# Differential attention: VectorE copies the turned probabilities out of PSUM, GpSimd forms the difference for the first 128 queries

## The chip, the cores and the metric

The kernel runs on one core of a Trainium2 chip. The metric is the device time of one execution in microseconds (us); the figure given is the median of three runs. The engines are named as the profile names them: TensorE (PE, with PEld for its weight loads), VectorE (DVE), ScalarE (ACT), GpSimd (POOL) and SyncE (SP). Each engine works through its own instructions in the order in which they are written, and semaphores hold one engine back for another.

## The reference, cut to what matters

The model is four transformer layers of width 1024 over 256 tokens, with an attention of one of three kinds between two feed-forward parts, and two more layers of another kind behind them. The change touches the two layers (the first and the fourth) that use differential attention: 8 heads, each with two sets of scores, whose softmaxes are subtracted before they meet the values.

```python
def diff_attention(h, w_in, w_out, lam, subln_g, lambda_init, pos):
    q, k, v = jnp.split(h @ w_in, 3, axis=-1)
    ...
    lam_full = jnp.exp(jnp.sum(lam[0] * lam[1])) - jnp.exp(jnp.sum(lam[2] * lam[3])) + lambda_init
    ...
        sc = jnp.einsum('bqhcd,bkhcd->bhcqk', qc, k, preferred_element_type=jnp.float32) * scale
        p = masked_probs(sc, pos[None, :] <= qpos[:, None])
        a = p[:, :, 0] - lam_full * p[:, :, 1]
        return jnp.einsum('bhqk,bkhe->bqhe', a.astype(v.dtype), v)

    o = chunked(chunk, S // Q_BLOCK)
    o = rms_norm(o, subln_g, DIFF_SUBLN_EPS) * (1.0 - lambda_init)
    return o.reshape(B, S, H * DIFF_V_DIM) @ w_out
```

## The kernel before, in words

Every engine's program is written by hand, and the order of the calls is the order of its instructions. Most of the time goes into large matrix products: the weights stream in by DMA, ScalarE and VectorE split each weight into a high and a low part (tiles HI and LO), and TensorE multiplies both. Between the input product of an attention and its output product (function `rows_of_outputs`, whose matmuls are at L826) lies the core of the attention, a pipeline over the 8 heads; the change lies there, in both differential layers.

In that core, for head i, TensorE computes two score matrices (`pair_scores`, L892, and the mask added at L900), into PSUM, of 384 columns each: columns 0 to 127 hold queries 0 to 127 against keys 0 to 127, columns 128 to 383 hold queries 128 to 255 against all 256 keys. VectorE finds the negated row maxima (`maxima`, tile NM, L2141 and L2142). ScalarE takes the exponentials into SBUF (`exps`, tile SB, L1614) with their row sums. VectorE inverts the sums (`reciprocals`, tile RC, L2146), makes one factor for each query (tile CF, L2192), and forms first set plus factor times second set in place, in two instructions (L2197): one over the 128 columns of the first group of queries, one over the other 256. TensorE turns the 128 by 128 blocks of the result (`probs_turned`, L706) into PSUM bank 4. ScalarE copies the turned blocks into SBUF (`probs`, tile PT, L1622). TensorE multiplies them with the values (`outputs`, L923; `mixed` in the program). ScalarE sums the squares of the output (`sums`, L1450), GpSimd makes the inverse root from them (`outputs_roots`, L2611 and L2613), and VectorE scales the output into its place (`in_place`, L2205 and L2208).

The heads overlap. TensorE's order in round i is: scores of head i+2, turn of head i, output of head i-1. VectorE's is: difference of head i, `in_place` of head i-3, maxima of head i+2. ScalarE's is: copy of head i, exponentials of head i+2, squares of head i-1. In round 7 TensorE also turns the finished first half of the output (`outputs_flipped`), which ScalarE and VectorE split into a high and a low part (`outputs_high`, `outputs_low`, tiles XH and XL). The output product at L826 begins when head 5 is in its place and this first half is split. GpSimd has done its part in moving queries and keys (`exchange`) long before; in the core it makes only the inverse roots.

Of the kernel before, what the change touches and what calls it, by code (L numbers as in the profile page):

```python
# [122 lines left out]
def build(nc, a, out, mods, turned, turned_qk):  # L123
    ctx = ExitStack()
    with ctx:
# [20 lines left out]
        def sem(name):  # L146
            return ctx.enter_context(nc.semaphore(name))
# [205 lines left out]
        s_cf = sem("s_cf")  # L353
        s_df = sem("s_df")
        s_d0 = sem("s_d0")
        s_p1 = sem("s_p1")
# [138 lines left out]
        for st in steps:  # L495
# [89 lines left out]
            "sc": pair, "ma": {"mix2": 4}, "nm": soft, "ex": soft, "rc": soft,  # L585
            "cf": {"diff": 8}, "df": {"diff": 8, "nsa": 16}, "p1": {"nsa": 16}, "d0": {"nsa": 16}, "pf": soft, "pt": soft, "mix": pair,
            "eq": {"diff": 16, "mix2": 16}, "ev": {"diff": 8, "mix2": 4}, "er": {"diff": 8, "mix2": 4},
# [10 lines left out]
        def bank_of(i):  # L598

            return (6, 4)[i] if i < 2 else 2 * ((i + 1) % 2)  # L600
# [96 lines left out]
        def _(e):  # L697
# [264 lines left out]
            def softmax_attention(st):  # L962
# [19 lines left out]
                for i in range(8):  # L982
                    if i + 2 < 8:

                        e.wait_ge(*((s_cp, c["cp"] + 5 + i) if i < 2 else (s_ex, c["ex"] + i + 1)))
                        if i == 2:
                            e.wait_ge(s_qt, c["qa"] + 4)
                        pair_scores(st, i + 2)
                    if i == 0:

                        e.wait_ge(s_ex, c["ex"] + 2)
                    if i == 7:

                        e.wait_ge(s_ex, c["ex"] + 8)
                        outputs_flipped(st, 0, 8 if diff else 4)
                    e.wait_ge(s_df if diff else s_ex, c["df" if diff else "ex"] + i + 1)
                    probs_turned(st, i, nj)
                    if i >= 1:
                        mixed(i - 1)
# [413 lines left out]
        def _(e):  # L1413
# [203 lines left out]

            def probs(st, i, nj):
                e.wait_ge(s_pf, st.c["pf"] + i + 1)
                if i >= 2:  # L1620
                    e.wait_ge(s_mix, st.c["mix"] + i - 1)
                e.activation(st.t["PT"][:, i % 2, 0:nj, :], ps[:, 4:4 + nj, 0:384], ACT.Copy).then_inc(s_pt, 1)  # L1622

# [9 lines left out]
            def diff_or_moba(st):  # L1633
# [29 lines left out]
                for i in range(8):  # L1663
                    if i == 7:
                        outputs_high(st, 0)
                    probs(st, i, 1 if diff else 2)
                    if i + 2 < 8:
                        exps(st, i + 2, bank_of(i + 2))
                    if diff and i >= 1:
                        sums(i - 1)  # L1670
# [196 lines left out]
        def _(e):  # L1867
# [297 lines left out]
            def diff(st):  # L2165
# [20 lines left out]
                def difference(i):  # L2186

                    reciprocals(st, i)
                    if i == 0:
                        e.wait_ge(s_lam, c["lam"] + 4)  # L2190
                    e.wait_ge(s_rc, c["rc"] + i + 1)
                    e.scalar_tensor_tensor(out=CF[:, i], in0=SM[:, i, :, 0], scalar=LS[:, 5:6], in1=RC[:, i, :, 1],  # L2192
                                           op0=ALU.mult, op1=ALU.mult).then_inc(s_cf, 1)
                    e.wait_ge(s_cf, c["cf"] + i + 1)
                    X = SB[:, i % 3]
                    for t, (c0, c1) in enumerate(((0, 128), (128, 384))):
                        o = e.scalar_tensor_tensor(out=X[:, 0, c0:c1], in0=X[:, 1, c0:c1], scalar=CF[:, i, t:t + 1],  # L2197
                                                   in1=X[:, 0, c0:c1], op0=ALU.mult, op1=ALU.add)
                    o.then_inc(s_df, 1)

# [13 lines left out]
                projected(st, 5, TM, 0, 0)  # L2214
                maxima(st, 2, bank_of(2))
                maxima(st, 3, bank_of(3))
                for i in range(2, 8):
                    difference(i)
                    if i >= 3:
                        in_place(i - 3)  # L2220
                    if i == 7:
                        outputs_low(st, 0)
                    if i + 2 < 8:
                        maxima(st, i + 2, bank_of(i + 2))
                for i in range(5, 8):
# [274 lines left out]
        def _(e):  # L2500
# [104 lines left out]

            def outputs_roots(st, width, eps, at, pairs):

                for i in range(pairs):
                    ss, v, r = (ST[:, at + 3 * width * i + j * width:at + 3 * width * i + (j + 1) * width] for j in range(3))
                    e.wait_ge(s_eq, st.c["eq"] + width * (i + 1))  # L2610
                    e.tensor_scalar(v, ss, 1.0 / P, eps, ALU.mult, ALU.add).then_inc(s_ev, 1)  # L2611
                    e.wait_ge(s_ev, st.c["ev"] + i + 1)
                    e.tensor_tensor(r, v, NH[:, 0:width], ALU.pow).then_inc(s_er, 1)  # L2613

            def diff(st):
# [5 lines left out]
                exchange(st, 4)  # L2621
                outputs_roots(st, 2, 1e-5, 32, 8)

# [25 lines left out]
            def mix2(st):  # L2649
# [8 lines left out]
                exchange(st, 2)  # L2658
                outputs_roots(st, 4, 1e-6, 32, 4)
                load_for(bounds[st.k + 1])  # L2660
# [50 lines left out]
```

## Time and profile before

| what | value |
| --- | --- |
| device time, median of 3 runs (lowest to highest) | 2737.24 us (2736.77 to 2737.26) |
| the profiled execution: span from first to last instruction | 2735.8 us |
| TensorE busy in it | 2707.6 us, 99% of the span |
| VectorE, ScalarE, GpSimd busy | 1939.9, 1541.6, 533.0 us |
| first differential layer's core, by the output product's start | up to 286.49 us |
| second differential layer's core, by the output product's start | up to 1761.85 us |

The span is the profiled execution's own time; the median of the runs lies 1.4 us above it, for what lies around the instructions. A busy share of 99% for TensorE is an average over the whole program: in the cores of the attentions it is lower, and what happens there is read from those stretches alone. Every time in the text below that has no other unit is in microseconds from the start of the span, or a duration in microseconds.

### The profile page before, as it was taken

How to read it: one execution, taken by the hardware profiler on the slowest of the kernel's cores; microseconds unless marked ns; L12 is line 12 of the kernel's file. 1: busy time of each engine (PE TensorE's matmuls, PEld its weight loads, DVE VectorE, ACT ScalarE, POOL GpSimd, SP SyncE). 2: the span in 40 equal slices, each digit the busy share in tenths (PEclk: the TensorE clock that was granted, in tenths of full speed). 3: DMA queues.
4: the chain of work that ended last, by engine and by line, in shares of the span. 5: the costliest groups of instructions: out<-in, count | busy, mean ns of one | idle time of the engine just before them, and what ended most of it. 6: DMA issues, size and time to landing. Idle time of an engine off the chain costs nothing.

```text
span 2735.8 us, 34478 instructions
## 1 busy us (share of the span) xinstructions
PE 2707.6 (99%) x12754; PEld 2216.3 (81%) x12754; DVE 1939.9 (71%) x2831; ACT 1541.6 (56%) x2646; POOL 533.0 (19%) x930
## 2 busy tenths in 40 slices
PE   9999999999999999999999999999999999999998
PEld 7887788888888888876888888788788788788787
DVE  6877777787667778767786787778764765745764
ACT  6547764654766465456654656765445444444543
POOL 3211221221112122115221211122110021110120
PEclk9999999999999999999999999999999999999999
DMA  9867488786748868661796886478675686764773
GB/s 293 288 229 256 155 273 281 223 280 234 254 144 275 288 215 281 242 211 50 226 292 226 272 305 226 155 250 292 238 238 186 202 264 219 247 196 166 235 244 114
DMA packets 386919, 633.87 MB, mean 232 GB/s; under 512 B 25760, under 2 KB 255136, under 8 KB 386496
## 3 DMA queue, kind: packets, MB, share of 16 engines
q1 hardware_dynamic: 350752, 535.02, 58.9%
q0 software_dynamic: 35856, 96.30, 11.0%
q8 instruction: 101, 1.65, 0.2%
q14 instruction: 66, 0.54, 0.1%
q10 hardware_dynamic: 144, 0.36, 0.0%
HBM read 593.26 MB, written 38.32 MB: 231 GB/s over the span
## 4 chain that ended last, share of the span: by engine, by line
PE 95%; DVE 3%; ACT 1%; issue 1%; POOL 0%; DMA 0%; DVEq 0%; ACTq 0%
PE ps L736 41%; PE ps L826 28%; PE ps L742 20%; PE ps L706 2%; PE ps L892 1%; PE ps L923 1%; PE ps L795 1%; ACT SB L1614 1%; PE ps L933 0%; DVE M L2026 0%; PE ps L900 0%; ACT JUNK L1450 0%; PE ps L1065 0%; DVE H L1972 0%; DVE M L1969 0%
## 5 line engine op out<-in xcount | busy, mean ns | idle before, releaser
L736 PE MATMUL ps<-HI,XH 128*128 128x512 f32 x2480 | 973.2, 392 | 1.7 <-DVE LO L1886 0.8
L736 PE MATMUL ps<-LO,XH 128*128 128x512 f32 x2480 | 966.5, 390 | 0.0
L1881 DVE TENSOR_TENSOR LO<-RAW,HI 128x1024 fp32r<-128x1024 f32 x468 | 564.6, 1218 | 328.9 <-ACT HI L1430 326.6
L742 PE MATMUL ps<-HI,XL 128*128 128x512 f32 x2480 | 767.5, 391 | 0.4
L1430 ACT ACTIVATE HI<-RAW 128x1024 fp32r<-128x1024 f32 x468 | 492.7, 1060 | 483.2 <-PE ps L826 279.5
L1886 DVE SCALAR_TENSOR_TENSOR LO<-RAW,GC,HI 128x512 fp32r<-128x512 f32 (+1 forms) x896 | 617.0, 742 | 142.2 <-ACT HI L1437 141.0
L1437 ACT ACTIVATE HI<-RAW,GC 128x512 fp32r<-128x512 f32 (+1 forms) x896 | 586.3, 713 | 206.5 <-PE ps L742 177.6
L736 PEld LDWEIGHTS ps<-HI,XH 128*128 128x128 f32 x2480 | 466.1, 188 | 103.4 <-DVE LO L1886 3.1
L742 PEld LDWEIGHTS ps<-HI,XL 128*128 128x128 f32 x2480 | 464.1, 188 | 105.2 <-DVE XL L1922 9.7
L736 PEld LDWEIGHTS ps<-LO,XH 128*128 128x128 f32 x2480 | 466.5, 188 | 94.5
L2583 POOL DMA_DIRECT2D AX<-turned x440 | 240.0, 552 | 351.3 <-DMA turned<-AT 302.9
L826 PE MATMUL ps<-HI,AH 128*128 128x512 f32 x856 | 265.2, 391 | 0.0
L826 PE MATMUL ps<-LO,AH 128*128 128x512 f32 x856 | 263.8, 389 | 0.0
L826 PE MATMUL ps<-HI,AL 128*128 128x512 f32 x856 | 263.8, 389 | 0.0
L826 PEld LDWEIGHTS ps<-HI,AL 128*128 128x128 f32 x856 | 160.7, 188 | 33.5
L826 PEld LDWEIGHTS ps<-LO,AH 128*128 128x128 f32 x856 | 160.7, 188 | 33.4
L826 PEld LDWEIGHTS ps<-HI,AH 128*128 128x128 f32 x856 | 159.6, 188 | 32.5
L2578 POOL DMA_DIRECT2D turned<-AT x110 | 61.9, 563 | 532.4 <-DVE AT L2087 532.4
L1566 ACT ACTIVATE SG<-ps,ST 128x256 f32<-128x256 f32 x176 | 73.7, 471 | 129.6 <-PE ps L742 129.6
L2529 POOL TENSOR_TENSOR ST<-ST,NH 128x1 f32<-128x1 f32 x56 | 34.5, 617 | 518.9 <-DVE ST L2005 263.5
L2078 DVE SCALAR_TENSOR_TENSOR AF<-ps,ST,SG 128x256 f32<-128x256 f32 x176 | 77.0, 480 | 80.2 <-ACT SG L1566 80.2
L1916 DVE SCALAR_TENSOR_TENSOR ACC<-RAW,CS,ACC 128x512 f32<-128x512 f32 x168 | 126.1, 751 | 5.1
(229 smaller groups left out, 2210.4 us busy)
## 6 DMA issues: line engine op xcount, KB each, us to landing
RAW<-in_ffn_w_in SPq DMA_DIRECT2D x350, 512.0 KB, 5.1
RAW<-in_ffn_w_out SPq DMA_DIRECT2D x88, 1024.0 KB, 6.2
RAW<-in_w_ada SPq DMA_DIRECT2D x48, 1024.0 KB, 6.6
RAW<-in_w_in SPq DMA_DIRECT2D x44, 1024.0 KB, 5.2
RAW<-in_w_ffn_in SPq DMA_DIRECT2D x88, 512.0 KB, 4.9
turned<-AT POOLq DMA_DIRECT2D x110, 256.0 KB, 2.6
AX<-turned POOLq DMA_DIRECT2D x440, 64.0 KB, 3.6
RAW<-in_diff_w_in SPq DMA_DIRECT2D x24, 1024.0 KB, 5.4
```

Source lines behind the costliest of these rows:

```text
L736: e.matmul(ps[:, b + t, 0:nw], XH[:, k, t * P:(t + 1) * P], q[s][:, c * nw:(c + 1) * nw], start=(k == 0 and q is HI), stop=False)
L742: i = e.matmul(ps[:, b + t, 0:nw], XL[:, k, t * P:(t + 1) * P], HI[s][:, c * nw:(c + 1) * nw], start=False, stop=(k == 7))
L826: i = e.matmul(ps[:, 4 + 2 * t + nh, :], x(k, t), q[s][:, nh * 512:nh * 512 + 512], start=(k == 0 and q is HI and x is th), stop=(k == chu ...
L1430: e.activation(HI[n % NSPLIT][:, 0:t.width], RAW[t.buf][:, h * t.width:(h + 1) * t.width], ACT.Copy).then_inc(s_hi, 1)
L1437: i = e.activation(HI[n % NSPLIT][:, c * w:(c + 1) * w], RAW[t.buf][:, h * t.width + c * w:h * t.width + (c + 1) * w], ACT.Copy, scale=g[c])
L1566: o = e.activation(SG[:, i, t], ps[:, b + t, 0:S], ACT.Silu, scale=r)
L1881: e.tensor_tensor(LO[n % NSPLIT][:, 0:w], RAW[t.buf][:, at[1] * w:(at[1] + 1) * w], HI[n % NSPLIT][:, 0:w].bitcast(F32), ALU.subtract).the ...
L1886: i = e.scalar_tensor_tensor(out=LO[n % NSPLIT][:, c * w2:(c + 1) * w2], in0=RAW[t.buf][:, at[1] * w + c * w2:at[1] * w + (c + 1) * w2], s ...
L1916: e.scalar_tensor_tensor(out=A, in0=src, scalar=CS[:, kc:kc + 1], in1=A, op0=ALU.mult, op1=ALU.add).then_inc(s_ada, 1)
L2078: o = e.scalar_tensor_tensor(out=AF[:, i, t], in0=ps[:, b + t, S:2 * S], scalar=root_of(st, t)[0], in1=SG[:, i, t], op0=ALU.mult, op1=ALU. ...
L2578: e.dma_start(rows, AT[:, g % 2, :]).then_inc(s_bw[g % 2], 16)
L2583: e.dma_start(AX[32 * c:32 * c + 32, g % 3, :].rearrange("p (q n) -> p q n", q=4), rows[:, c * P:(c + 1) * P].rearrange("(q j) n -> j q n" ...
```

## The change

Three pieces of work change hands in the two differential layers. The copy of the turned probabilities out of PSUM goes from ScalarE to VectorE (`turned_copied`), behind the maxima of head i+2. The difference of the first 128 queries goes from VectorE to GpSimd, where it takes two instructions with a wait between them: a scaling in place of the second set's 128 columns, then an addition. TensorE's turn of a head now waits for both engines. In VectorE's order the maxima of head i+2 come before `in_place` of head i-3, where they came behind it. GpSimd makes the roots of head i-2 behind the difference of head i. Nothing else moves; the result is the same sum.

```diff
@@ TensorE, softmax_attention
                     e.wait_ge(s_df if diff else s_ex, c["df" if diff else "ex"] + i + 1)
+                    if diff:
+                        e.wait_ge(s_d0, c["d0"] + i + 1)
                     probs_turned(st, i, nj)
@@ ScalarE, diff_or_moba
                 for i in range(8):
                     if i == 7:
                         outputs_high(st, 0)
-                    probs(st, i, 1 if diff else 2)
+                    if not diff:
+                        probs(st, i)
@@ VectorE, diff
                     X = SB[:, i % 3]
-                    for t, (c0, c1) in enumerate(((0, 128), (128, 384))):
-                        o = e.scalar_tensor_tensor(out=X[:, 0, c0:c1], in0=X[:, 1, c0:c1], scalar=CF[:, i, t:t + 1],
-                                                   in1=X[:, 0, c0:c1], op0=ALU.mult, op1=ALU.add)
-                    o.then_inc(s_df, 1)
+                    e.scalar_tensor_tensor(out=X[:, 0, 128:384], in0=X[:, 1, 128:384], scalar=CF[:, i, 1:2],
+                                           in1=X[:, 0, 128:384], op0=ALU.mult, op1=ALU.add).then_inc(s_df, 1)
+
+                def turned_copied(i):
+
+                    e.wait_ge(s_pf, c["pf"] + i + 1)
+                    if i >= 2:
+                        e.wait_ge(s_mix, c["mix"] + i - 1)
+                    e.tensor_copy(x["PT"][:, i % 2, 0, :], ps[:, 4, 0:384]).then_inc(s_pt, 1)
...
                 maxima(st, 2, bank_of(2))
+                turned_copied(0)
                 maxima(st, 3, bank_of(3))
+                turned_copied(1)
                 for i in range(2, 8):
                     difference(i)
+                    if i + 2 < 8:
+                        maxima(st, i + 2, bank_of(i + 2))
+                    turned_copied(i)
                     if i >= 3:
                         in_place(i - 3)
                     if i == 7:
                         outputs_low(st, 0)
-                    if i + 2 < 8:
-                        maxima(st, i + 2, bank_of(i + 2))
@@ GpSimd, diff
-                outputs_roots(st, 2, 1e-5, 32, 8)
+                SB, CF = st.t["SB"], st.t["CF"]
+                for i in range(10):
+                    if i < 8:
+
+                        e.wait_ge(s_cf, st.c["cf"] + i + 1)
+                        X = SB[:, i % 3]
+                        e.tensor_scalar(X[:, 1, 0:P], X[:, 1, 0:P], CF[:, i, 0:1], None, ALU.mult).then_inc(s_dm, 1)
+                        e.wait_ge(s_dm, st.c["cf"] + i + 1)
+                        e.tensor_tensor(X[:, 0, 0:P], X[:, 0, 0:P], X[:, 1, 0:P], ALU.add).then_inc(s_d0, 1)
+                    if i >= 2:
+                        output_roots(st, 2, 1e-5, 32, i - 2)
```

VectorE's instructions for head 5 in the first differential layer stood as follows before the change. RC, SM and CF are reciprocals, row sums and factors, SB the exponentials, M the output.

```order
L2146 RECIPROCAL RC_99<-SM_98 128x4 [waits s_ex]
L2192 SCALAR_TENSOR_TENSOR CF_104<-SM_98,LS_106,RC_99 128x2 [waits s_rc]
L2197 SCALAR_TENSOR_TENSOR SB_95<-SB_95,CF_104 128x128 [waits s_cf]
L2197 SCALAR_TENSOR_TENSOR SB_95<-SB_95,CF_104 128x256
L2205 TENSOR_TENSOR ST<-ST,RC_99 128x2 [waits s_er]
L2208 SCALAR_TENSOR_TENSOR M<-ps,ST,SGN_107 128x128 [waits s_ef]
L2208 SCALAR_TENSOR_TENSOR M<-ps,ST,SGN_107 128x128
L2141 TENSOR_REDUCE NM_97<-ps 128x2 [waits s_sc]
L2142 TENSOR_REDUCE NM_97<-ps 128x2
```

The same round of the changed kernel on VectorE (its own line numbers):

```order
L2150 RECIPROCAL RC_99<-SM_98 128x4 [waits s_ex]
L2196 SCALAR_TENSOR_TENSOR CF_104<-SM_98,LS_106,RC_99 128x2 [waits s_rc]
L2200 SCALAR_TENSOR_TENSOR SB_95<-SB_95,CF_104 128x256 [waits s_cf]
L2145 TENSOR_REDUCE NM_97<-ps 128x2 [waits s_sc]
L2146 TENSOR_REDUCE NM_97<-ps 128x2
L2208 COPY PT_96<-ps 128x384 [waits s_mix,s_pf]
L2214 TENSOR_TENSOR ST<-ST,RC_99 128x2 [waits s_er]
L2217 SCALAR_TENSOR_TENSOR M<-ps,ST,SGN_107 128x128 [waits s_ef]
L2217 SCALAR_TENSOR_TENSOR M<-ps,ST,SGN_107 128x128
```

One of the two instructions on SB is gone, the two maxima have moved ahead, and a copy that waits for TensorE's turn of the same head (s_pf) stands in the middle of the round, with `in_place` and the next head's difference behind it.

On GpSimd, the first differences of a layer now stand directly behind the last DMAs that `exchange` issues, where the first root stood.

```order
L2610 DMA turned_qk<-AT_102 128x1024 [waits s_qa]
L2615 DMA AX_103<-turned_qk 32x4x256 [waits s_qw,s_qt]
L2615 DMA AX_103<-turned_qk 32x4x256 x3
L2639 TENSOR_SCALAR SB_95<-SB_95,CF_104 128x128 [waits s_cf]
L2641 TENSOR_TENSOR SB_95<-SB_95 128x128 [waits s_dm]
```

Eight such pairs of a TENSOR_SCALAR and a TENSOR_TENSOR are new in each of the two layers, and from the third on the two instructions of a root follow each pair.

## Rows read from the trace of the kernel before

**Rows 1.** The page's first line.
```profile
span 2735.8 us, 34478 instructions
```

**Rows 2.** Stretches: length, busy PE, PEld, DVE, ACT, POOL (instructions), clock, DMA share, GB/s.
```profile
274.00:280.00 6.00, 3.94 (x34) 2.96 (x34) 5.75 (x20) 6.00 (x30) 2.27 (x5) 1.00 0.00 0
280.00:284.00 4.00, 3.42 (x17) 3.42 (x18) 3.12 (x12) 3.59 (x16) 1.49 (x5) 0.60 0.00 0
1750.00:1756.00 6.00, 3.95 (x34) 2.96 (x34) 5.75 (x20) 6.00 (x30) 2.27 (x5) 1.00 0.01 1
```

**Rows 3.** Chain that ended last, first layer: start, us, what.
```profile
279.78 0.76 DVE SB L2197 x2
...
280.58 0.76 PE ps L706 x3
```

**Rows 4.** Timeline, second layer, round 5: start, us, instruction, [idle before <-releaser].
```profile
1752.24 0.53 ACT L1622 ACTIVATE PT<-ps 128x384 f32<-128x384 f32 x1
1752.72 0.37 ACT L1614 ACTIVATE SB<-ps,NM 128x128 f32<-128x128 f32 x1
1752.75 0.22 DVE L2192 SCALAR_TENSOR_TENSOR CF<-SM,LS,RC 128x2 f32<-128x2 f32 x1
1753.01 0.75 DVE L2197 SCALAR_TENSOR_TENSOR SB<-SB,CF 128x128 f32<-128x128 f32 x2
1753.27 0.48 DVE L2197 SCALAR_TENSOR_TENSOR SB<-SB,CF 128x256 f32<-128x256 f32 x1
1753.67 0.15 DVE L2205 TENSOR_TENSOR ST<-ST,RC 128x2 f32<-128x2 f32 x1
1753.81 0.55 PE L706 MATMUL ps<-CST,SB 128*128 128x128 f32 x3 [0.35 <-DVE SB L2197]
1754.39 0.41 DVE L2141 TENSOR_REDUCE NM<-ps 128x2 f32<-128x256 f32 x1
1755.31 0.17 DVE L2146 RECIPROCAL RC<-SM 128x4 f32<-128x4 f32 x1
1755.52 0.22 DVE L2192 SCALAR_TENSOR_TENSOR CF<-SM,LS,RC 128x2 f32<-128x2 f32 x1
```

**Rows 5.** Timelines of another attention's core: VectorE's copy, GpSimd's scalings, what overlaps.
```profile
1242.48 0.17 DVE L2276 TENSOR_TENSOR CG<-RC,GS 128x4 f32<-128x4 f32 x1
1242.74 1.02 POOL L2646 TENSOR_SCALAR SB<-SB,CG 128x256 f32<-128x256 f32 x1 [0.87 <-DVE CG L2276]
1243.74 0.60 POOL L2646 TENSOR_SCALAR SB<-SB,CG 128x128 f32<-128x128 f32 x1
...
1245.56 0.55 DVE L2286 COPY PT<-ps 128x384 f32<-128x384 f32 x1
1246.03 0.41 DVE L2141 TENSOR_REDUCE NM<-ps 128x2 f32<-128x256 f32 x1
1247.00 0.92 POOL L2646 TENSOR_SCALAR SB<-SB,CG 128x256 f32<-128x256 f32 x1
1247.38 0.41 DVE L2346 TENSOR_TENSOR PC<-PC,MC 128x240 f32<-128x240 f32 x1
```

**Rows 6.** GpSimd's groups by form: count, busy us, mean ns, idle before.
```profile
L2613 POOL TENSOR_TENSOR ST<-ST,NH 128x2 f32<-128x2 f32 x16 | 11.2, 700 | 1.3
L2611 POOL TENSOR_SCALAR ST<-ST 128x2 f32<-128x2 f32 x16 | 3.1, 193 | 58.8 <-ACT JUNK L1450 58.7
```

**Rows 7.** Timeline: head 2's factor and the output product's start, both layers; XL.
```profile
268.57 0.22 DVE L2192 SCALAR_TENSOR_TENSOR CF<-SM,LS,RC 128x2 f32<-128x2 f32 x1
286.49 0.47 PE L826 MATMUL ps<-HI,XH 128*128 128x512 f32 x1 [0.17 <-issue]
1744.57 0.22 DVE L2192 SCALAR_TENSOR_TENSOR CF<-SM,LS,RC 128x2 f32<-128x2 f32 x1
1759.76 1.28 DVE L1922 TENSOR_TENSOR XL<-ps,XH 128x512 fp32r<-128x512 f32 x2
1761.85 0.47 PE L826 MATMUL ps<-HI,XH 128*128 128x512 f32 x1 [0.53 <-issue]
```

More of the change, by code:

```diff
@@ L354, in build @@
         s_df = sem("s_df")
+        s_dm = sem("s_dm")
         s_d0 = sem("s_d0")
@@ L585, in build @@
             "sc": pair, "ma": {"mix2": 4}, "nm": soft, "ex": soft, "rc": soft,
-            "cf": {"diff": 8}, "df": {"diff": 8, "nsa": 16}, "p1": {"nsa": 16}, "d0": {"nsa": 16}, "pf": soft, "pt": soft, "mix": pair,
+            "cf": {"diff": 8}, "df": {"diff": 8, "nsa": 16}, "p1": {"nsa": 16}, "d0": {"diff": 8, "nsa": 16}, "pf": soft, "pt": soft, "mix": pair,
             "eq": {"diff": 16, "mix2": 16}, "ev": {"diff": 8, "mix2": 4}, "er": {"diff": 8, "mix2": 4},
@@ L1616, in exps, with probs @@
                 o.then_inc(s_ex, 1)
-            def probs(st, i, nj):
+            def probs(st, i):
                 e.wait_ge(s_pf, st.c["pf"] + i + 1)
@@ L1621, in probs @@
                     e.wait_ge(s_mix, st.c["mix"] + i - 1)
-                e.activation(st.t["PT"][:, i % 2, 0:nj, :], ps[:, 4:4 + nj, 0:384], ACT.Copy).then_inc(s_pt, 1)
+                e.activation(st.t["PT"][:, i % 2], ps[:, 4:6, 0:384], ACT.Copy).then_inc(s_pt, 1)
             def outputs_high(st, half):
@@ L2604, in exchange, with output_roots @@
                                     turned_qk[q][:, c * S:(c + 1) * S].rearrange("(q j) n -> j q n", q=4)).then_inc(sem_r, 16)
[L2606 to L2613, printed above, removed]
+            def output_roots(st, width, eps, at, i):
+                ss, v, r = (ST[:, at + 3 * width * i + j * width:at + 3 * width * i + (j + 1) * width] for j in range(3))
+                e.wait_ge(s_eq, st.c["eq"] + width * (i + 1))
+                e.tensor_scalar(v, ss, 1.0 / P, eps, ALU.mult, ALU.add).then_inc(s_ev, 1)
+                e.wait_ge(s_ev, st.c["ev"] + i + 1)
+                e.tensor_tensor(r, v, NH[:, 0:width], ALU.pow).then_inc(s_er, 1)
             def diff(st):
@@ L2658, in mix2 @@
                 exchange(st, 2)
-                outputs_roots(st, 4, 1e-6, 32, 4)
+                for i in range(4):
+                    output_roots(st, 4, 1e-6, 32, i)
                 load_for(bounds[st.k + 1])
```

## The prediction, as it was put on record before the run

> **What bounds the kernel now.** I started from the page: the span is 2735.8 us [rows 1], so one profiled execution lies 1.4 us under the median of 2737.24, and the sum below is made against the span and carried over with those 1.4. TensorE is busy nearly all the time, so a change in an attention's core counts only as far as it lengthens or shortens TensorE's idle time there. Next I asked for busy time by stretch in the cores of the two layers [rows 2]. In the steady part of the first (274 to 280) TensorE works 3.94 of 6.00 us, VectorE 5.75 and ScalarE 6.00; the second layer shows the same three numbers. TensorE is not the bound there; VectorE and ScalarE are both nearly full. The chain that ended last goes in the first layer from VectorE's difference straight to TensorE's turn [rows 3]: the turn waits for VectorE.
>
> Which of the two full engines sets the pace is seen in one round of the timeline [rows 4]. VectorE's starts follow each other without a gap: factor at 1752.75, difference at 1753.01 and 1753.27, in_place at 1753.67, maxima at 1754.39, reciprocal at 1755.31, next factor at 1755.52. The steps are 0.26, 0.26, 0.40, 0.72, 0.92 and 0.21; they add up to the round of 2.77 us. Nothing in that list waits for another engine, while TensorE's turn sat idle 0.35 us for VectorE's difference. ScalarE's copy and what it waits for take 0.48 of its round (1752.24 to 1752.72). So VectorE sets the pace and ScalarE is close behind.
>
> **The change part by part.** ScalarE loses the copy, 0.48 us per head. As ScalarE follows VectorE, this by itself is worth nothing on the path.
>
> VectorE loses the 128-column difference, a step of 0.26 [rows 4], and gains a copy of 128x384 from PSUM. The very same copy stands in another attention's core: it takes 0.55, and the next instruction starts 0.47 after it [rows 5]. So VectorE's own work goes from 2.77 to 2.77 - 0.26 + 0.47 = 2.98 per round, on the engine that sets the pace, before any wait.
>
> The larger part is a new wait. The copy of head i stands in VectorE's queue before in_place and the next head's difference, and it needs TensorE's turn of the same head, which now needs GpSimd too. Let T be the start of the factor CF of head i.
> - The factor is ready at T + 0.22 [rows 4]. GpSimd starts 0.09 after a VectorE result (1242.48 + 0.17 to 1242.74) [rows 5]: T + 0.31.
> - The scaling: GpSimd's TENSOR_SCALAR with a factor per row takes 0.60 over 128 columns when it follows another; over 256 columns 1.02 as the first after a wait against 0.92 otherwise, so 0.10 more for the first [rows 5]. 0.70: T + 1.01. Its own wait costs another hop of 0.09: T + 1.10.
> - The addition of two 128-column tiles stands nowhere in this trace. From below: a TENSOR_SCALAR over 2 columns with constants takes 0.19. From above: it reads as many elements as the 256-column scaling, 1.02 after a wait [rows 5, 6]. In between lies the fixed 0.19 plus 126 columns at the slope of the scalings, (0.92 - 0.60)/128 = 0.0025 us each, which is 0.51; GpSimd's only two-tile operation, a power over 2 columns, takes 0.70 [rows 6], but a power works more per element than an addition. I take 0.55: T + 1.65.
> - TensorE starts 0.05 after what it waits for (1753.01 + 0.75 to 1753.81) and takes 0.55 to turn three blocks [rows 4]: T + 2.25. With the same hop of 0.05 VectorE's copy starts at T + 2.30.
>
> VectorE, for its part, comes to the copy at T + 0.26 + 0.40 + 0.92 = T + 1.58. It stands 0.72 idle. From the copy: 0.47, in_place 0.72, reciprocal 0.21: the next factor starts at T + 3.70. The round grows from 2.77 to 3.70. That the maxima were moved ahead of in_place gives the wait a cover of 0.92; without it the idle time would be 1.64. In rounds 6 and 7 there are no maxima to cover it, and the round does not get shorter by them as it does now. Late next are TensorE's output of the head, which needs the copied tile, and at the end of the core the output product. The roots that now stand behind each pair on GpSimd cost nothing: the pair and a root (0.19 and 0.70 [rows 6]) fill 2.4 of 3.7 us, and in_place uses a root two rounds later. The first two copies stand behind maxima which wait for TensorE's scores anyway, with GpSimd idle; I cost them at nothing, and if that cover were gone they would cost 0.5 each.
>
> The length of a core, from the factor of head 2 to the first matmul of the output product, is now 286.49 - 268.57 = 17.92 in the first layer and 1761.85 - 1744.57 = 17.28 in the second [rows 7]. After the change: round 2 has no in_place, so 3.70 - 0.72 = 2.98; rounds 3 to 6 take 3.70 each, together 17.78 to the factor of head 7. From there: copy done and in_place of head 4 by 3.49, the low halves 1.28 (XL, [rows 7]), in_place of head 5 0.72, and some 0.1 for its end and the hop: 5.6. In all 23.4. That is 5.5 more in the first layer and 6.1 more in the second, 11.6 together.
>
> The granted clock is the last term. In the first layer's core it reads 0.60 on average from 280 to 284, right behind the stretch in which TensorE was busy 3.94 of 6.00 [rows 2]. The two levels are 1.2 and 2.4 GHz, so some 3.2 of these 4 us ran at the lower one. The second layer's stretch with the same activity stayed at 1.00 [rows 2], and its core is 0.64 shorter. After the change TensorE is idle more, in both layers. I take a fall in both, at 1 us each, and take off the 0.64 already paid: 1.4 more. The bounds are nothing (0.64 won back) and 1.6 in each layer, if all of such a fall lay in TensorE's own work.
>
> Sum: 2735.8 + 11.6 + 1.4 = 2748.8 for the span, and with the 1.4 around it 2750 us, slower by 0.5%.
>
> **The rivals.** *The scaling starts later.* VectorE's remaining difference reads two tiles from SBUF and starts 0.05 before GpSimd's scaling. If one shuts the other out of SBUF, the scaling begins only at its end, T + 0.74 instead of T + 0.31; with 0.43 in six places (five rounds and the end) of two layers that is 5.2 more: 2755. Against it: VectorE's operation on two SBUF tiles at 1247.38 takes 0.41 and lies wholly inside a scaling of GpSimd's (1247.00 to 1247.92), which takes 0.92 as the one behind another does [rows 5]. The Trainium skill (SBUF — State Buffer, Who interferes with whom) states that a VectorE instruction with two SBUF inputs and a GpSimd instruction that reads SBUF exclude each other, the one issued first blocking the other. By that rule the result would be this rival's; the pair at 1247.38 does not bear it out.
>
> *No new wait matters.* If the pair were done in 0.62, TensorE's turn would end before VectorE reaches its copy, and only VectorE's own 2.98 would count: rounds of 2.26, three of 2.98 and one of 2.06, together 13.3, and an end of 4.7: 18.0, which is 0.1 and 0.7 more than now. With the clock as it is: 2738. Against it: the scaling alone takes 0.70.
>
> *Faster.* ScalarE also shows 6.00 of 6.00 [rows 2], and if it set the pace, its 0.48 less would shorten the five rounds from 2.77 to 2.29 in each of two layers, 4.8, and its copy of the last head would leave the end, another 0.5 each: 2731.5. It decides from the point where VectorE's round falls below 2.77, so it needs both a pair under 0.62 and a copy step under 0.26, where the rows show 0.70 and 0.47.
>
> *The clock stays low longer*, into the output product: beyond 1.6 a layer, over 2757.
>
> For the addition's own price the Trainium skill has a figure: GPSIMD Engine Reference, Elementwise — side-by-side cycle accounting, gives 4497 ns for such an addition over 2048 columns, which scaled to 128 is an estimate of 0.28 us without a fixed cost. By it the sum would be 0.27 x 12 = 3.2 less, 2747; no row here shows it.
>
> **How the numbers follow.** Forecast 0.74, the scaling shut out 0.14, no wait 0.06, faster 0.03, a longer low clock 0.03. About 0.2%, 5.5 us, is what a measurement of this kernel can tell from no change. The addition between 0.19 and 1.02 moves the sum by -0.36 x 12 = -4.3 and +0.47 x 12 = +5.6; the clock by -2.0 and +1.2. Both ends at once give 2743.7 to 2756.8; I give 2743 to 2757, which holds the shut-out scaling too and leaves out no wait, faster and the long low clock. Slower 0.74 + 0.14 + 0.03 = 0.91; the same 0.06; faster 0.03.
>
> **What would show it.** In the changed profile: VectorE's copy idle about 0.7 us before most heads and 1.6 in rounds 6 and 7, released by TensorE's turn; the turn released by GpSimd's addition, not by VectorE; the pair at 0.70 and about 0.55; factors 3.7 apart; the output product 23 us behind head 2's factor; ScalarE with idle time. I am wrong in size if the addition lies far from 0.55, and in kind if the copies wait for nothing or if factors come under 2.77 apart.

## The result, and the profile after

The changed kernel takes 2752.4 us (median of 5 runs, 2751.13 to 2755.0) against 2737.24 before: a ratio of 1.0056, with a 95% interval of 1.0045 to 1.0067. It is slower by 15.2 us, or 0.56%. The forecast was 2750, with a range of 2743 to 2757. The profiled execution took 2753.32, with a span of 2751.5. The five runs differ in the granted clock, too: the two with a mean of 0.998 took 2751.13 and 2751.18, the three with 0.996 took 2752.4 to 2755.0; the profile is of one of these three.

The page's first lines for the changed kernel: span, then busy time, share of the span and instructions of each engine.

```profile
span 2751.5 us, 34494 instructions
PE 2711.4 (99%) x12754; PEld 2217.6 (81%) x12754; DVE 1943.8 (71%) x2831; ACT 1537.2 (56%) x2630; POOL 555.7 (20%) x962
```

The span is 15.7 longer than in [rows 1], yet TensorE's and VectorE's busy times grew by only 3.8 and 3.9; GpSimd's grew by 22.7 with its new pairs. Most of the time went into waiting. One round of the first layer's core (head 4) in the timeline (start, duration, instruction, idle before and what ended it) shows the wait. It answers to [rows 4]. Here and in all timelines below, the rows that matter are picked out and those between them left out.

```profile
274.91 0.22 DVE L2196 SCALAR_TENSOR_TENSOR CF<-SM,LS,RC 128x2 f32<-128x2 f32 x1
275.16 0.48 DVE L2200 SCALAR_TENSOR_TENSOR SB<-SB,CF 128x256 f32<-128x256 f32 x1
275.23 0.90 POOL L2639 TENSOR_SCALAR SB<-SB,CF 128x128 f32<-128x128 f32 x1 [1.40 <-DVE CF L2196]
275.57 0.41 DVE L2145 TENSOR_REDUCE NM<-ps 128x2 f32<-128x256 f32 x1
276.20 0.45 POOL L2641 TENSOR_TENSOR SB<-SB 128x128 f32<-128x128 f32 x1
276.76 0.52 PE L707 MATMUL ps<-CST,SB 128*128 128x128 f32 x3 [1.41 <-issue]
277.31 0.56 DVE L2208 COPY PT<-ps 128x384 f32<-128x384 f32 x1 [0.73 <-PE ps L707]
278.70 0.22 DVE L2196 SCALAR_TENSOR_TENSOR CF<-SM,LS,RC 128x2 f32<-128x2 f32 x1
```

Read it as a ring: factor 274.91, scaling 275.23, addition 276.20, turn 276.76, copy 277.31, and after `in_place` and the reciprocal the next factor at 278.70. The round is 3.79 where it was 2.77. VectorE stands idle 0.73 before its copy, and TensorE 1.41 before its turn.

The end of the first layer's core in the same view, with head 2's factor and the output product's start in both cores, answers to [rows 7].

```profile
268.03 0.22 DVE L2196 SCALAR_TENSOR_TENSOR CF<-SM,LS,RC 128x2 f32<-128x2 f32 x1
284.36 0.87 PE L707 MATMUL ps<-CST,SB 128*128 128x128 f32 x3 [2.61 <-POOL SB L2641]
285.27 0.56 DVE L2208 COPY PT<-ps 128x384 f32<-128x384 f32 x1 [2.02 <-PE ps L707]
286.69 1.94 PE L707 MATMUL ps<-CST,M 128*128 128x128 f32 x8 [0.17 <-DVE M L2217]
289.43 0.56 DVE L2208 COPY PT<-ps 128x384 f32<-128x384 f32 x1 [2.03 <-PE ps L707]
292.71 0.96 PE L827 MATMUL ps<-HI,XH 128*128 128x512 f32 x2 [0.96 <-issue]
1752.75 0.22 DVE L2196 SCALAR_TENSOR_TENSOR CF<-SM,LS,RC 128x2 f32<-128x2 f32 x1
1777.42 0.70 PE L827 MATMUL ps<-HI,XH 128*128 128x512 f32 x2 [0.96 <-issue]
```

Here the releaser of the turn is named, GpSimd's addition. Without maxima to cover it, VectorE's idle time before its copies of heads 6 and 7 is 2.02 and 2.03. The cores are 292.71 - 268.03 = 24.68 and 1777.42 - 1752.75 = 24.67 long, where they were 17.92 and 17.28: 14.15 of the 15.7.

Busy time by stretch of the first layer (length; busy time of PE, PEld, DVE, ACT, POOL; granted clock; DMA) answers to [rows 2].

```profile
274.00:280.00 6.00, 3.73 (x35) 2.54 (x33) 5.05 (x18) 4.25 (x22) 3.13 (x5) 1.00 0.00 0
280.00:284.00 4.00, 1.19 (x9) 1.03 (x9) 2.40 (x8) 2.42 (x12) 2.42 (x5) 0.84 0.01 4
284.00:290.00 6.00, 5.47 (x26) 4.97 (x26) 2.60 (x9) 2.00 (x6) 3.37 (x7) 0.54 0.00 0
293.00:297.00 4.00, 4.00 (x12) 3.12 (x11) 2.22 (x6) 0.55 (x1) 0.65 (x1) 0.58 0.03 8
```

VectorE and ScalarE, both full before, now work 5.05 and 4.25 of 6.00. Behind the stretch in which TensorE was busy only 1.19 of 4.00, the clock reads 0.54, mostly its lower level of 1.2 GHz. The turn of head 6 took 0.87 there, against 0.52 above. The output product, too, ran at 0.58 from 293 to 297.

The rest of the 15.7 lies outside the cores. Head 2's factor came 0.54 earlier in the first layer, the way from its output product to the second core grew from 1458.08 to 1460.04, and the way from the second output product to the end of the span from 973.95 to 974.08: -0.54 + 6.76 + 1.96 + 7.39 + 0.13 = 15.70.

### The profile page after: what moved, and what is told of

Same layout as the page of the kernel before. It is cut to its first block, busy times and chain, and to the rows that moved or that the text cites. A ratio compares the mean times of both kernels' runs of the same rounds, so it can differ in the third digit from the quotient of the medians.

```text
span 2751.5 us, 34494 instructions
## 1 busy us (share of the span) xinstructions
PE 2711.4 (99%) x12754; PEld 2217.6 (81%) x12754; DVE 1943.8 (71%) x2831; ACT 1537.2 (56%) x2630; POOL 555.7 (20%) x962
## 3 DMA queue, kind: packets, MB, share of 16 engines
q8 instruction: 101, 1.65, 0.2%
## 4 chain that ended last, share of the span: by engine, by line
PE 95%; DVE 3%; issue 1%; ACT 0%; POOL 0%; DMA 0%; SPq 0%; DVEq 0%; ACTq 0%
PE ps L737 40%; PE ps L827 28%; PE ps L743 20%; PE ps L707 2%; PE ps L893 1%; PE ps L924 1%; PE ps L796 1%; PE ps L901 0%; PE ps L934 0%; DVE M L2030 0%; DMA RAW<-in_ffn_w_in 0%; PE ps L1068 0%; DVE H L1976 0%; DVE PT L2208 0%; DVE M L1973 0%
```

## The experiments

The theory of the prediction is the chain: the copy holds VectorE until factor, scaling, addition and turn of the same head are done. The rival is load: VectorE simply has more to do, or GpSimd disturbs the others. The first four kernels tell these apart. The next ones ask why GpSimd's scaling took 0.90 instead of 0.70, and what the clock cost. The median of before lay between 2737.11 and 2737.58 beside them.

### The copy back on ScalarE

```diff
-            def probs(st, i):
+            def probs(st, i, nj):
...
-                    if not diff:
-                        probs(st, i)
+                    probs(st, i, 1 if diff else 2)
...
-                turned_copied(0)
                 maxima(st, 3, bank_of(3))
-                turned_copied(1)
...
-                    turned_copied(i)
```

> The copy goes back to ScalarE; GpSimd's pair and the order with the maxima first stay. Core means the length from the factor of head 2 to the first matmul of the output product (before 17.9 and 17.3, changed kernel 24.7 in both). Theory of the chain (VectorE's copy waits for GpSimd's pair and TensorE's turn, with the rest of VectorE's queue behind it): with no copy in VectorE's queue that wait is gone, but TensorE's turn still waits for the pair, and the scores of a later head stand behind it in TensorE's queue: core about 20, in all 2741.5, up to 2744 if the clock falls. Rival, load (VectorE is slower only because it carries more work, 2.98 a round instead of 2.77): its round falls to 2.51, so 2737 or less.

2741.8 (2740.88 to 2742.71), ratio 1.0015 [1.0006, 1.0025]. GpSimd's pair takes as long as in the changed kernel in most rounds, but no VectorE instruction waits for the turn, and 11 of the 15 us are gone. Load falls. The chain itself, with nothing queued behind it on VectorE, costs 4.2. Its timeline also showed a scaling that took less:

```profile
271.88 0.60 POOL L2635 TENSOR_SCALAR SB<-SB,CF 128x128 f32<-128x128 f32 x1
274.67 0.48 DVE L2199 SCALAR_TENSOR_TENSOR SB<-SB,CF 128x256 f32<-128x256 f32 x1
274.73 0.90 POOL L2635 TENSOR_SCALAR SB<-SB,CF 128x128 f32<-128x128 f32 x1
```

GpSimd came late to the one at 271.88, when VectorE's difference of that head was over (270.80 + 0.49).

### The difference back on VectorE

```diff
-                    if diff:
-                        e.wait_ge(s_d0, c["d0"] + i + 1)
...
-                    e.scalar_tensor_tensor(out=X[:, 0, 128:384], in0=X[:, 1, 128:384], scalar=CF[:, i, 1:2],
-                                           in1=X[:, 0, 128:384], op0=ALU.mult, op1=ALU.add).then_inc(s_df, 1)
+                    for t, (c0, c1) in enumerate(((0, 128), (128, 384))):
+                        o = e.scalar_tensor_tensor(out=X[:, 0, c0:c1], in0=X[:, 1, c0:c1], scalar=CF[:, i, t:t + 1],
+                                                   in1=X[:, 0, c0:c1], op0=ALU.mult, op1=ALU.add)
+                    o.then_inc(s_df, 1)
...
-                        e.tensor_scalar(X[:, 1, 0:P], X[:, 1, 0:P], CF[:, i, 0:1], None, ALU.mult).then_inc(s_dm, 1)
-                        e.wait_ge(s_dm, st.c["cf"] + i + 1)
-                        e.tensor_tensor(X[:, 0, 0:P], X[:, 0, 0:P], X[:, 1, 0:P], ALU.add).then_inc(s_d0, 1)
```

> VectorE forms the whole difference again; only the copy stays with VectorE. Chain: the turn follows VectorE's difference at once and is done before VectorE has finished the maxima, so the copy waits for nothing in rounds with maxima; VectorE's own round is 2.77 + 0.47 = 3.24; core about 20.3, in all 2742.7, up to 2745 with a low clock. Load: 3.24 is more work on VectorE than the changed kernel's 2.98, so slower than the changed kernel: 2754 or more.

2745.01 (2744.17 to 2745.2), ratio 1.0027 [1.0016, 1.0038], at the upper end of what the chain expects. VectorE's own work is now the largest of all these kernels, and the kernel is still 7 us faster than the changed one.

```profile
273.94 0.22 DVE L2194 SCALAR_TENSOR_TENSOR CF<-SM,LS,RC 128x2 f32<-128x2 f32 x1
275.79 0.55 DVE L2208 COPY PT<-ps 128x384 f32<-128x384 f32 x1
277.18 0.22 DVE L2194 SCALAR_TENSOR_TENSOR CF<-SM,LS,RC 128x2 f32<-128x2 f32 x1
282.05 0.56 DVE L2208 COPY PT<-ps 128x384 f32<-128x384 f32 x1 [0.64 <-PE ps L707]
```

In the rounds that have maxima the copy waits for nothing, and the round is 3.24: the old 2.77 plus the copy's step of 0.47. In rounds 6 and 7, which have none, the copy waits 0.64 and 1.52 for the turn even so, where it waits 2.02 and 2.03 in the changed kernel. So each half of the change costs 4.2 and 7.4 alone, and both together 15.2: 3.6 more than their sum. In the rounds with maxima the copy's wait exists only when the copy stands in VectorE's queue and the chain runs through GpSimd; in the last two rounds GpSimd makes it longer.

### The copy behind `in_place`

```diff
-                    turned_copied(i)
                     if i >= 3:
                         in_place(i - 3)
+                    turned_copied(i)
                     if i == 7:
                         outputs_low(st, 0)
```

> As the changed kernel, but VectorE's copy of head i stands behind in_place of head i-3 instead of before it: the same work on every engine, 0.72 more cover for the wait. Chain: the copy's wait of 0.7 goes in rounds that have maxima, rounds alternate between 3.1 and 3.6 instead of 3.8, core about 21.4 instead of 24.7, in all 2745 to 2748. Load: no change, 2752.

2746.29 (2745.49 to 2746.74), ratio 1.0032 [1.0021, 1.0044]. VectorE's list is the same as in the changed kernel, only with 0.72 more work ahead of the wait, and 6 us come back. This is load held constant and cover changed; the chain had said 2745 to 2748.

```profile
276.96 0.55 DVE L2208 COPY PT<-ps 128x384 f32<-128x384 f32 x1
```

This is the copy of head 4: it waits for nothing, and so do those of heads 3 and 5. In rounds 6 and 7 the wait is 1.31 and 1.49.

### The addition alone on GpSimd

```diff
-                        e.tensor_scalar(X[:, 1, 0:P], X[:, 1, 0:P], CF[:, i, 0:1], None, ALU.mult).then_inc(s_dm, 1)
-                        e.wait_ge(s_dm, st.c["cf"] + i + 1)
```

> GpSimd leaves out the scaling, so for the first 128 queries the second set is added unscaled; the addition stays. Chain: the pair gets 0.99 shorter and the copy no longer waits where there are maxima; rounds of 3.0, core about 19.5, in all 2741 to 2744. Load: no change, since VectorE does the same work: 2752. If GpSimd and VectorE shut each other out of SBUF, the addition, now beside VectorE's difference, takes longer than the 0.45 that it takes in the changed kernel.

2745.77 (2745.7 to 2748.87), ratio 1.0033 [1.002, 1.0046]. Against load, but some 2 us above what I had expected of the chain. Its timeline shows what the expectation lacked (the profile is of the run that took 2748.87):

```profile
268.46 0.78 DVE L2200 SCALAR_TENSOR_TENSOR SB<-SB,CF 128x256 f32<-128x256 f32 x1
268.50 0.45 POOL L2639 TENSOR_TENSOR SB<-SB 128x128 f32<-128x128 f32 x1 [6.40 <-DVE CF L2196]
271.06 0.48 DVE L2200 SCALAR_TENSOR_TENSOR SB<-SB,CF 128x256 f32<-128x256 f32 x1
271.21 0.64 POOL L2639 TENSOR_TENSOR SB<-SB 128x128 f32<-128x128 f32 x1
```

Where GpSimd's addition starts 0.04 behind VectorE's difference, the addition keeps its 0.45 and VectorE takes 0.78 instead of 0.48. Where it starts 0.15 behind, VectorE keeps its 0.48 and the addition takes 0.64. One of the two is held up, and which one hangs on a tenth of a microsecond. With VectorE's 0.30 more, the round of 2.98 comes to 3.28, and the factors show 3.26 (274.06, 277.32, 280.58). In this run the output products also began at the lower clock; whether they did in the other four is not shown. The Trainium skill (SBUF — State Buffer, Who interferes with whom) says: "Issue order, not op shape, decides who blocks." This trace does not bear that out by the starts that it shows: VectorE starts first both times, and is held up by 0.30 in the one case and GpSimd by 0.19 in the other.

### VectorE's difference behind the maxima

```diff
                                            op0=ALU.mult, op1=ALU.mult).then_inc(s_cf, 1)
+
+                def rest(i):
+
                     e.wait_ge(s_cf, c["cf"] + i + 1)
...
                     if i + 2 < 8:
                         maxima(st, i + 2, bank_of(i + 2))
+                    rest(i)
                     turned_copied(i)
```

> The changed kernel with one thing moved: VectorE's own part of the difference (256 columns) stands behind the maxima of head i+2 instead of ahead of them. GpSimd's scaling waits for the same factor as before, but while it runs VectorE reads PSUM (maxima) and not two tiles in SBUF. Theory A, the scaling takes 0.90 instead of 0.60 because VectorE's two-tile instruction shuts it out for a while: the scaling falls to 0.60 to 0.70. Theory B, it takes 0.90 because it is the first instruction behind a wait: it stays at 0.87 to 0.92. Under A the turn is ready soon after VectorE's own part (factor + 1.65) and rounds are about 3.7; under B the addition ends at factor + 1.9 and rounds are 3.8 to 3.9. Time under A 2750 to 2753, under B 2752 to 2756; the durations tell more than the time here.

2754.91 (2754.17 to 2755.9), ratio 1.0063 [1.0046, 1.008]: slower than I had expected under theory A, and in the range of theory B. The durations are the answer:

```profile
276.88 0.22 DVE L2196 SCALAR_TENSOR_TENSOR CF<-SM,LS,RC 128x2 f32<-128x2 f32 x1
277.20 0.61 POOL L2645 TENSOR_SCALAR SB<-SB,CF 128x128 f32<-128x128 f32 x1 [2.52 <-DVE CF L2196]
277.36 0.42 DVE L2145 TENSOR_REDUCE NM<-ps 128x2 f32<-128x256 f32 x1 [0.25 <-PE ps L901]
277.89 0.45 POOL L2647 TENSOR_TENSOR SB<-SB 128x128 f32<-128x128 f32 x1
278.30 0.48 DVE L2203 SCALAR_TENSOR_TENSOR SB<-SB,CF 128x256 f32<-128x256 f32 x1
278.83 0.55 PE L707 MATMUL ps<-CST,SB 128*128 128x128 f32 x3 [1.51 <-DVE SB L2203]
285.06 0.89 POOL L2645 TENSOR_SCALAR SB<-SB,CF 128x128 f32<-128x128 f32 x1 [1.78 <-DVE CF L2196]
```

The scaling waits for the factor as before and takes 0.61 beside the maxima, which read PSUM. In rounds 6 and 7, which have no maxima, VectorE's difference stands beside it again, and it takes 0.89 and 0.90 in the same kernel. So theory B, that the wait makes it long, falls. The time rose because the maxima waited 0.25 for scores, and then VectorE's own part was what the turn waited for.

### What VectorE reads meanwhile

Two kernels replace VectorE's part of the difference by something shorter. The first leaves out the factor:

```diff
-                    e.scalar_tensor_tensor(out=X[:, 0, 128:384], in0=X[:, 1, 128:384], scalar=CF[:, i, 1:2],
-                                           in1=X[:, 0, 128:384], op0=ALU.mult, op1=ALU.add).then_inc(s_df, 1)
+                    e.tensor_tensor(X[:, 0, 128:384], X[:, 0, 128:384], X[:, 1, 128:384], ALU.add).then_inc(s_df, 1)
```

> The changed kernel, but VectorE's own part of the difference adds the second set without its factor for queries 128 to 255 (a TENSOR_TENSOR of two SBUF tiles instead of a SCALAR_TENSOR_TENSOR); the factor is left out there. It starts beside GpSimd's scaling as before. Theory A, two tiles of SBUF read by VectorE shut GpSimd's scaling out for a while: the scaling stays at 0.85 to 0.92. Theory C, the factors, which both engines then read from the same small tile, are what holds the scaling up: it falls to 0.60 to 0.65 and rounds to 3.5.

2750.88 (2750.81 to 2751.09), ratio 1.005 [1.0034, 1.0066].

```profile
275.21 0.42 DVE L2200 TENSOR_TENSOR SB<-SB 128x256 f32<-128x256 f32 x1
275.27 0.83 POOL L2638 TENSOR_SCALAR SB<-SB,CF 128x128 f32<-128x128 f32 x1 [1.40 <-DVE CF L2196]
```

The second leaves out the second set:

```diff
-                    e.scalar_tensor_tensor(out=X[:, 0, 128:384], in0=X[:, 1, 128:384], scalar=CF[:, i, 1:2],
-                                           in1=X[:, 0, 128:384], op0=ALU.mult, op1=ALU.add).then_inc(s_df, 1)
+                    e.tensor_scalar(X[:, 0, 128:384], X[:, 0, 128:384], CF[:, i, 1:2], None, ALU.mult).then_inc(s_df, 1)
```

> The changed kernel, but VectorE's own part scales the first set by the factor for queries 128 to 255 and reads the second set not at all (a TENSOR_SCALAR of one SBUF tile); that part of the difference is left out. Theory A, it is VectorE's second SBUF tile that shuts GpSimd out: the scaling falls to 0.60 to 0.65 though VectorE's instruction still overlaps it and reads the same small tile of factors, and rounds fall to about 3.5, the time to 2748 to 2751. Theory C, the shared tile of factors: it stays at 0.85 to 0.92 and the time at 2751 to 2753.

2749.68 (2749.49 to 2750.15), ratio 1.0046 [1.003, 1.0062].

```profile
275.35 0.35 DVE L2200 TENSOR_SCALAR SB<-SB,CF 128x256 f32<-128x256 f32 x1
275.41 0.76 POOL L2638 TENSOR_SCALAR SB<-SB,CF 128x128 f32<-128x128 f32 x1 [1.32 <-DVE CF L2196]
```

Theory C falls: without a factor on VectorE the scaling is not back at 0.60. Theory A falls as I had put it: with a single tile (and the small one of factors) on VectorE it is not either. What holds is simpler. The scaling ends 0.47 behind the end of VectorE's instruction in both (275.63 to 276.10, 275.70 to 276.17), and 0.49 behind it in the changed kernel (275.64 to 276.13). Of its 0.60 some 0.11 to 0.13 pass beside VectorE's instruction, and the rest comes when that has ended. The Trainium skill (same page and section) states that a VectorE tensor_scalar between SBUF tiles can run in a mode in which it blocks GpSimd too; the 0.76 of the second kernel agrees with that.

In all of these VectorE and GpSimd work on parts of one tile, SB, so a clash within that tile would be a rival. A row of the changed kernel speaks against it: ahead of head 2, GpSimd's addition of head 1 runs into a large VectorE instruction on three other tiles.

```profile
261.91 1.36 DVE L1885 TENSOR_TENSOR LO<-RAW,HI 128x1024 fp32r<-128x1024 f32 x1
262.52 1.07 POOL L2641 TENSOR_TENSOR SB<-SB 128x128 f32<-128x128 f32 x1
```

The addition takes 1.07 instead of 0.45 and ends 0.32 behind VectorE's end (263.27 to 263.59): again all of it but 0.13.

### The clock kept up

Matmuls whose result nobody reads fill TensorE's idle time. The first try put them ahead of the wait for VectorE:

```diff
+                    if diff and 2 <= i < 7:
+                        e.wait_ge(s_pt, c["pt"] + i)
+                        for _ in range((0, 0, 4, 4, 8, 8, 16)[i]):
+                            e.matmul(ps[:, 4, 384:512], ident, cst("mask")[:, 0:P], start=True, stop=True)
                     e.wait_ge(s_df if diff else s_ex, c["df" if diff else "ex"] + i + 1)
```

> The changed kernel with matmuls on TensorE whose result nobody reads (4, 4, 8, 8 and 16 of 128 columns in rounds 2 to 6, into a free part of PSUM bank 4), between the scores and the turn, where TensorE waits for the difference. Nothing that VectorE, ScalarE or GpSimd do is changed. Theory, the rounds of 3.8 come from the chain factor, scaling, addition, turn, copy, and the lower clock comes on top through the turn of head 7, the flips and the output product: rounds stay at 3.75 to 3.85, the granted clock stays at 1.00 in the cores, the cores come to 23.9 to 24.2 instead of 24.7 and the first layer's output product starts at full speed, so 2749 to 2750.5. Rival, TensorE is itself late in this chain: then rounds grow with the added matmuls and the time rises above 2753. Rival, the lower clock costs nothing here: 2752 to 2753 as the changed kernel.

2754.63 (2753.28 to 2755.74), ratio 1.0063 [1.0047, 1.0078]. It missed its aim: 8 and 16 of them were too many, the rounds grew to 4.03 and 4.82 because TensorE came late to its turn, and the gain from the clock was lost in that. Fewer of them, in a better place:

```diff
+                def kept_busy(n):
+                    for _ in range(n):
+                        e.matmul(ps[:, 4, 384:512], ident, cst("mask")[:, 0:P], start=True, stop=True)
...
+                    if diff and i == 6:
+                        e.wait_ge(s_pt, c["pt"] + i)
+                        kept_busy(5)
                     e.wait_ge(s_df if diff else s_ex, c["df" if diff else "ex"] + i + 1)
                     if diff:
+                        if i >= 2:
+                            kept_busy(4)
                         e.wait_ge(s_d0, c["d0"] + i + 1)
...
                 mixed(7)
+                if diff:
+                    kept_busy(4)
```

> The changed kernel with fewer matmuls on TensorE whose result nobody reads (4 of 128 columns in each of rounds 2 to 7, behind VectorE's part of the difference and ahead of the wait for GpSimd's; 5 more in round 6, where the last scores are gone, and 4 behind the last head's output). Four take about 0.7, and TensorE waits there for GpSimd from factor + 0.8 to factor + 1.85, so they fit. Theory, the lower clock costs on top of the chain: rounds stay at 3.75 to 3.85, the clock stays at 1.00 in both cores and behind them, the turn of head 7 falls from 0.87 to 0.52 and the flips from 1.9 to 1.0, the cores come to 23.6 to 24.2, and the time to 2748.5 to 2750.5. Rival, the added matmuls still delay the turn, as 8 and 16 did: rounds over 3.9 and 2752 or more. Rival, the time lost at the lower clock is hidden: cores 24.5 to 24.8 and 2752 to 2753 although the clock reads 1.00.

2750.67 (2750.46 to 2751.02), ratio 1.0049 [1.0032, 1.0066]; its span is 2749.2. The median lies 0.2 above the range that I had given. The same stretches as above for the changed kernel:

```profile
280.00:284.00 4.00, 3.78 (x28) 3.38 (x29) 2.93 (x9) 2.42 (x12) 2.44 (x5) 1.00 0.00 0
284.00:290.00 6.00, 5.05 (x42) 4.63 (x41) 2.79 (x10) 2.02 (x7) 3.80 (x8) 1.00 0.00 0
293.00:297.00 4.00, 4.00 (x19) 3.28 (x18) 2.00 (x5) 0.32 (x1) 0.42 (x1) 1.00 0.11 14
```

and three rows of its timeline:

```profile
268.54 0.22 DVE L2207 SCALAR_TENSOR_TENSOR CF<-SM,LS,RC 128x2 f32<-128x2 f32 x1
285.41 0.56 DVE L2219 COPY PT<-ps 128x384 f32<-128x384 f32 x1 [1.65 <-PE ps L707]
292.48 0.70 PE L827 MATMUL ps<-HI,XH 128*128 128x512 f32 x2
```

The clock stays at 1.00, the rounds behind the first at 3.78 to 3.85, and the core is 23.94 long in both layers instead of 24.7. The span is 2.3 shorter, the median 1.7; all four runs (2750.46 to 2751.02) lie under all five of the changed kernel. What remains of the core's growth is the chain and VectorE's own 0.21 more a round, and VectorE's idle time in round 6 is 1.65, not 2.02.

### The order of the maxima alone

The kernel before, with only the maxima moved ahead of `in_place`:

```diff
                     difference(i)
+                    if i + 2 < 8:
+                        maxima(st, i + 2, bank_of(i + 2))
                     if i >= 3:
                         in_place(i - 3)
                     if i == 7:
                         outputs_low(st, 0)
-                    if i + 2 < 8:
-                        maxima(st, i + 2, bank_of(i + 2))
```

> The kernel before with only the third piece of the change: VectorE's maxima of head i+2 stand ahead of in_place of head i-3. Copy and difference stay where they were. Theory, the order by itself costs and gives nothing, since VectorE's list is the same and full, so rounds stay at 2.77 and the time at 2736.5 to 2738.5. Rival, it makes ScalarE's exponentials start earlier and the time falls by over 2 us, or the maxima wait for scores that aren't there yet and it rises by over 2 us.

2737.02 (2736.51 to 2737.65), ratio 0.9998 [0.9989, 1.0008]. This piece of the change costs and gives nothing by itself.

## Why the prediction was right, and where its sum was off

**The mechanism** was right and is shown by the experiments: the copy put a wait for a chain through GpSimd and TensorE into the queue of the engine that sets the pace. Taking the copy out of that queue gives 11 us back, taking GpSimd out of the chain 7, and more cover ahead of the copy 6.

**The steps of the round**, with T the start of the factor, in the round shown above. GpSimd starts at T + 0.32 (forecast 0.31). The scaling takes 0.90 (forecast 0.70), and its own hop 0.07 (0.09). The addition takes 0.45 (0.55): the estimate by the slope was high, and nearer than either bound. TensorE starts 0.11 behind it (0.05), at T + 1.85, and VectorE's copy at T + 2.40 (2.30). From there to the next factor it is 1.39 (1.40). The round is 3.79 instead of 3.70: the scaling's +0.20 is half made up by the addition's -0.10, and the small terms cancel. VectorE's idle time is 0.73 (0.72). That it agrees so well is luck: the copy starts 0.10 later than forecast, but VectorE, too, comes to it 0.09 later (T + 1.67, forecast 1.58). In rounds 6 and 7, at full clock, the idle time is 1.65 (1.6).

**The rival that was set aside** is the step that failed. I priced the scaling at 0.60 plus 0.10 "for the first after a wait", and gave its being shut out by VectorE 14 in 100, because at 1247.38 the two overlap without harm [rows 5]. The 0.10 was not from a wait. In the trace of before, one row that the prediction did not draw on stands just ahead of that scaling of 1.02 at 1242.74:

```profile
1242.68 0.29 DVE L2279 TENSOR_SCALAR SB<-SB,CG 128x128 f32<-128x128 f32 x1
```

It ends at 1242.97, and the scaling ends 0.79 behind it, which is its undisturbed 0.92 less the same 0.13 as in the two kernels with a shorter instruction on VectorE. The shut-out was in the rows, and it scales with VectorE's instruction: 0.10 for one of 0.29, 0.30 for one of 0.48. The rival had the mechanism right and its price too high (0.43, against 0.30 measured), since some 0.13 passes beside. At 1247.38 GpSimd's scaling had been running for 0.38 when VectorE's instruction came; why neither was longer there, no run here tells. So the account is shown for a GpSimd scaling that starts 0.06 or more behind VectorE's instruction; a VectorE instruction that comes second is open.

**The cores.** With the clock at 1.00 both are 23.94, forecast 23.4: 0.08 to 0.15 more in each round and 0.08 at the end.

**The clock.** It fell in both layers, as forecast. In the cores of the profiled run that cost 49.35 - 47.88 = 1.47 in all, where I had taken 2.0. But I then took off the 0.64 that the first layer had lost before. That was an error of the sum: the difference of the core lengths, 23.4 - 17.92, already had it in it. And I had given only 3 in 100 to a low clock that reaches into the output product: in the first layer it did (0.58 from 293 to 297), and most of the 1.96 that the way to the second core grew lies there. With the clock kept up, that way grew by 0.37. Over all the traces the split is clean: in the three in which the lower clock reaches into the first output product (the changed kernel, the addition alone, and the first try at the clock) the way is 1460.02 to 1460.04 long, in the other nine 1458.01 to 1458.49.

Together, for the profiled span, the forecast was 13.0 more and 15.7 came. The chain was short by 1.08, the double deduction by 0.64, the output product's stretch and the tail by 2.09; the clock in the cores was 0.53 too dear, and 0.54 came from the earlier start of the first core, which I had set at nothing. 1.08 + 0.64 + 2.09 - 0.53 - 0.54 = 2.74. That start lies between 267.96 and 268.54 in the other kernels with an edit, so no cause of the 0.54 is shown. The 1.4 that I carried from the span to the time compared a median with the span of one run; each run of the changed kernel lies 1.8 above its own span.

The *no new wait* rival falls by the idle 0.73, and the *long low clock* by the time, though in the profiled run the low clock did reach into the output product. The *faster* rival falls because ScalarE, without its copy, was not the pace: it now works 4.25 of 6.00. The 0.28 that was worked out for the addition from the Trainium skill (GPSIMD Engine Reference, Elementwise — side-by-side cycle accounting) is not borne out: it took 0.45.

## What to carry to other kernels

Before work is moved off a full engine, look at what the engine will then wait for: here 0.26 of VectorE's work a round went away and 0.47 came, but of the 14.15 by which the two cores grew, VectorE's busy time makes up 3.05 and its idle time 11.1. Most of the idle time stands before the copies (6.1 of the 7.45 in the first core, 0.2 to 2.0 each), and everything queued behind a copy waits with it. An instruction that waits for a round trip through other engines belongs behind as much of the queue's own work as there is. When a duration in the trace is longer than its twin's, look for what ran on the other engines in that moment before it is put down to a start-up cost.

## What the runs showed of the hardware that was not expected

VectorE's instruction on SBUF tiles holds up a GpSimd scaling that starts 0.06 to 0.07 behind it until it ends, but for 0.11 to 0.13: 0.90, 0.83 and 0.76 beside instructions of 0.48, 0.42 and 0.35, against 0.60 alone. The tiles need not be the same: an addition of 0.45 took 1.07 beside a VectorE instruction on others. That a single large SBUF tile on VectorE does it too I had not expected. Where a GpSimd addition starts only 0.04 behind VectorE's instruction, it is VectorE that is held up (0.78 instead of 0.48).

TensorE's idle time has a price of its own: four idle-filling matmuls a round (nine in round 6, four more behind the last head) kept the granted clock at 1.00 in both cores and took 1.7 us off the median without moving any other engine's work.
